# Gathering the last two channel blocks of expert 0's tokens between the two halves of its gate products

## The reference

```python
hdn = (silu(einsum('nd,edf->nef', xt, w_gate[gi])) * einsum('nd,edf->nef', xt, w_up[gi]))
hdn = hdn * comb[:, gi, :, None]          # weight of each token for each expert, mostly zero
y = y + einsum('nef,efd->nd', hdn, w_down[gi])
```

## Time and profile before

| | before |
|---|---|
| median of 3 runs | 772.37 us (772.29 to 773.62) |
| the profiled execution, its own time | 772.13 us |
| its span in the profile | 770.4 us |
| TensorE busy | 750.6 us, 97% of the span |
| weights read | 240.56 MB in all, mean 312 GB/s |
| granted TensorE clock | 0.998 |

### The profile page before, as it was taken

The page is one execution under the profiler, slowest core; times in us unless marked ns, Lnnn a source line. Parts: engine busy times, 40 slices in busy tenths (PEclk is TensorE's granted clock), DMA queues, the critical chain, the costliest instruction groups (busy, mean ns, idle before and its releaser), DMA issues.

```text
span 770.4 us, 16167 instructions
## 1 busy us (share of the span) xinstructions
PE 750.6 (97%) x6544; PEld 538.9 (70%) x6544; DVE 323.0 (42%) x795; ACT 311.6 (40%) x632; POOL 124.9 (16%) x209
## 2 busy tenths in 40 slices
PE   8999999999999999999999999999999999998995
PEld 8989989998999988755555555565555555455552
DVE  4895787678675855712211311221222113012112
ACT  6976678576684744712112121222112121111123
POOL 7473242225423640000000000000000000000000
PEclk9999999999999999999999999999999999999999
DMA  8537554554754479999999999999999999999993
GB/s 206 148 86 194 149 145 131 138 151 111 191 140 125 153 241 327 374 407 421 427 424 430 426 428 427 429 424 428 425 428 427 427 429 424 430 426 428 422 415 127
DMA packets 83265, 240.56 MB, mean 312 GB/s; under 512 B 7281, under 2 KB 65762, under 8 KB 69746
## 3 DMA queue, kind: packets, MB, share of 16 engines
q1 hardware_dynamic: 82882, 238.67, 81.4%
q10 hardware_dynamic: 304, 0.79, 0.4%
HBM read 238.40 MB, written 1.05 MB: 311 GB/s over the span
## 4 chain that ended last, share of the span: by engine, by line
PE 83%; DMA 11%; DVE 3%; issue 2%; ACT 1%; SPq 0%; DVEq 0%
PE banks L2218 24%; PE banks L1863 22%; PE banks L2276 12%; DMA ring<-in_expert_w_up_dram 10%; PE banks L2142 3%; PE banks L2231 3%; PE banks L2060 3%; PE banks L1983 1%; PE banks L1996 1%; PE banks L2252 1%; PE banks L2044 1%; PE banks L2000 1%; PE banks L1987 1%; DMA room<-in_w_in_dram 1%; PE banks L2021 1%
## 5 line engine op out<-in xcount | busy, mean ns | idle before, releaser
L2218 PE MATMUL banks<-ring,bench 128*64 128x256 f32 x2016 | 235.6, 388 | 5.1 <-DMA ring<-in_expert_w_up_dram 3.6
L2218 PEld LDWEIGHTS banks<-ring,bench 128*64 128x64 f32 x2016 | 144.5, 134 | 102.6 <-issue 19.5
L1863 PE MATMUL banks<-rounded 128*128 128x256 f32 (+2 forms) x1320 | 193.5, 293 | 0.4 <-DVE room L1481 0.4
L1863 PEld LDWEIGHTS banks<-rounded 128*128 128x128 f32 x1320 | 168.0, 188 | 3.7 <-issue 0.6
L1762 DVE TENSOR_TENSOR bench<-banks,bench 128x256 f32<-128x256 f32 x32 | 13.6, 424 | 254.3 <-PE banks L2218 182.7
L2276 PE MATMUL banks<-ring,bench 128*64 128x512 f32 x512 | 116.9, 598 | 0.3 <-ACT bench L1144 0.3
L1155 ACT ACTIVATE ysb<-banks 64x512 f32<-64x512 f32 x63 | 37.3, 592 | 150.3 <-PE banks L2276 149.5
L2276 PEld LDWEIGHTS banks<-ring,bench 128*64 128x64 f32 x512 | 33.9, 136 | 62.8 <-issue 60.2
L923 ACT ACTIVATE rounded<-room 128x1024 fp32r<-128x1024 f32 x64 | 67.4, 1054 | 22.1 <-PE banks L1863 15.0
L1144 ACT ACTIVATE bench<-banks 128x256 f32<-128x256 f32 x32 | 12.3, 385 | 142.8 <-PE banks L2252 142.8
L1381 DVE TENSOR_TENSOR rounded<-room,rounded 128x1024 fp32r<-128x1024 f32 x49 | 62.4, 1273 | 15.2 <-ACT rounded L923 14.2
(11 more groups left out here) (317 smaller groups left out, 876.4 us busy)
## 6 DMA issues: line engine op xcount, KB each, us to landing
ring<-in_expert_w_down_dram SPq DMA_DIRECT2D x27, 2048.0 KB, 24.8
ring<-in_expert_w_up_dram SPq DMA_DIRECT2D x25, 2048.0 KB, 26.9
ring<-in_expert_w_gate_dram SPq DMA_DIRECT2D x24, 2048.0 KB, 25.9
room<-in_w_in_dram SPq DMA_DIRECT2D x56, 512.0 KB, 4.0
ring<-in_expert_w_gate_dram SPq DMA_DIRECT2D x10, 1024.0 KB, 9.8
ring<-in_expert_w_up_dram SPq DMA_DIRECT2D x8, 1024.0 KB, 10.4
ring<-in_expert_w_up_dram SPq DMA_DIRECT2D x12, 512.0 KB, 6.5
ring<-in_expert_w_down_dram SPq DMA_DIRECT2D x6, 1024.0 KB, 8.7
```

The lines of the kernel that those rows point to most:

```text
L1863: ins = T.matmul(o, a, b[:, k, lo_at:L], start=(k == 0 and n == 0), stop=(k == KT - 1 and n == 2))
L2218: ins = T.matmul(pb[5 + c][half * 64:half * 64 + SLOTS, 0:256], xgT[:, q % ROOMS, kt, j * SLOTS:(j + 1) * SLOTS], ws[kt // 4][:, kt % 4, h ...
```

## The change

TensorE now runs parts 0 to 2 of the first gather, starts gate 0's products with channel blocks 0 to 3, then gathers part 3, and then runs gate 0's blocks 4 to 7. On VectorE `weigh` goes ahead of `bring(0, 3)`. The number of instructions stays the same, and no semaphore is added or taken away.

```diff
                     bring(0, 1)
+                    weigh()
                     bring(0, 3)
-                    weigh()
                     weighed()
                     settle()
...
                 def gather_first():
...
                             ins = products(xlo, part, t)
                             if t == TT - 1:
                                 ins.then_inc(S("gathered"), 1)
+                def gather_last_part():
+
                     for t in range(TT):
                         products(xhi, PARTS - 1, t)
                     for t in range(TT):
...
                     for kt in range(KT):
+                        if first and c == 0 and kt == KT // 2:
+                            gather_last_part()
                         if first and c == 0 and kt % 4 == 0:
                             pe.wait_ge(S("xgT_side"), kt // 4 * 2 + 2)
```

More of the change, by code:

```diff
@@ L2153, in spread_gain, with products @@
                     ins.then_inc(S("gathered"), 1)
-                def gather_first():
[L2157 to L2165, removed]
+                per = KT // PARTS
+                def products(x, part, t):
+                    for k in range(per):
+                        ch = (part * per + k) * P
+                        ins = T.matmul(pb[FIRST_BANK[part]][:, k * WIDE:(k + 1) * WIDE], x[:, t, ch:ch + P], hot[:, t, :],
+                                       start=(k == 0 and t == 0 and x is xhi), stop=(t == TT - 1 and x is xlo), skip_group_check=True)
+                    return ins
+                def gather_first():
                     for t in range(TT):
```

## The result

The changed kernel takes 773.93 us (median of 22 runs, 772.14 to 774.86), the kernel before 772.47 us (22 runs, 771.99 to 774.21). The ratio is 1.0016, 95% interval 1.0010 to 1.0021: slower by 1.46 us at the medians, which is clear of zero. It is 0.19%, just inside the 0.2% (1.5 us) that the prediction took for the least that can be told from no change, and the interval reaches 0.21%. The forecast was 772.0 us, with a range up to 773.6.

A forecast was written before the change was run, and what follows sets the result against it. The weight stream was taken to bound the end. Profiled 772.13 us less 0.36 for the earlier first release gave 771.8; the runs' median lying 0.24 above the profiled execution made it 772.0 us, range 771.3 to 773.6.

The forecast's parts named there:

- What bounds the kernel: From 340 us on the weight stream sets the end; TensorE delays before 612 us are made up if no hole opens.
- its three cases: Whole-kernel time against 772.37 us: same 0.88 (within 1.5 us), faster 0.05, slower 0.07.
- Gate 0's start and the first release: TensorE starts gate 0 at 322.40 after idling about 0.68 us; half 1 of chunk 9 is issued 0.36 us earlier.
- Gate 0's end: Gate 0 on TensorE ends at 327.22 instead of 326.54, 0.68 us later.
- The wait at kt = 6: Blocks 6 and 7 wait for VectorE's part 3, ready 0.09 us before wanted: cost nothing, 0.85 us if not hidden.
- VectorE: Moved weigh costs nothing; the chain behind bring(0, 3) ends at about 329.4, hidden with 2 us left.
- the clock: Rival at gate 0: idle TensorE drops from 2.4 to 1.2 GHz, giving about 776.3 us; chance 0.04.
- The SP queue: Half 1 of chunk 9 issues 0.36 us earlier, everything behind 0.68 later; the stream still passes 0.36 us to the end.
- the 4.8 us of the first load: Landing time of half 1 of chunk 9, taken as alone in an empty queue; later loads took 6.4 and 6.7.
- My second reading: At half 0 of chunk 10, 2.2 us from issue to full rate leaves a 0.2 us hole, over half the gain.
- My sign of being wrong: Landings of 4.8 us for the halves of chunk 10 would mean that their issue sets the stream.
- the second half's issue sets the stream: Rival at the 329 us hand-over: up to 0.68 us slower, 0.2 more with a VectorE wait, 772.5 to 773.3; chance 0.21.

The follow-up runs named there:

- the long delay: Kernel before with 24 idle gather matmuls put between gate 0's halves: 776.28 us, ratio 1.0048 (1.0032 to 1.0064).

## Why the prediction was wrong

What bounds the kernel was right: the end follows the weight stream, TensorE's own delay before 612 us costs nothing by itself, and the loss of the first 340 us is still there at the end. By the prediction's own bound of 0.2% the result is "same", the likeliest of its three cases, but barely, and not for the reason given; the sign and the time were wrong, and the median lies 0.3 us above the range.

*Gate 0's start and the first release.* Right in kind: 322.44 against 322.40 forecast, the idle 0.62 us against 0.68, the release 0.28 earlier against 0.36.

*Gate 0's end.* Mis-sized: 1.00 us late against 0.68. Gate 0 began 0.78 us after the place where part 3 had begun (322.44 less 321.72 - 0.06, the shift of the traces) where I had 0.68; part 3 took 1.12 us between the halves against 1.04, and each half 1.96 against 1.89. The last two I take for the price of changing once more between gathers and products, which the working left out; no run tests that.

*The wait at kt = 6, VectorE, the clock.* Right: no idle there, `weigh` is free, and PEclk stayed at 1.00 through the 0.62 us. The Trainium skill, "TensorE: Matmul & The Clock Gate" (Part 1), says that the throttled clock is the default and activity releases it; at this pause no fall shows.

*The SP queue.* This is the step that failed: "by its own issue it could land at 327.33 + 4.8", so that the stream would stay the later of the two and "the 0.36 us pass through it to the end". I took the 4.8 us of the first load as the floor for one that follows another, and all above it as waiting that a later issue would use up. I worked that out for three loads, up to half 1 of chunk 10, and went from there to the end. For half 0 of chunk 10, the hand-over that I looked at, the bytes show no loss. By the same rule half 1 of chunk 11, which landed after 6.4 us before, would have had 1.6 us to spare. In its place the runs showed that it had none: with its issue 0.54, 1.00, 1.28 or 3.21 us later, the stream was 0.66, 1.41, 1.67 or 3.17 us later from there on, while releases ahead of it gained nothing by coming earlier. The 4.8 us were not those of a load in an empty queue either: half 0 of chunk 9, issued at 315.37, was still landing until 326.87, two microseconds after half 1 was issued:

```profile
spare<-in_expert_w_gate_dram SPq DMA_DIRECT2D x1, 1024.0 KB, 11.5
```

My second reading, a hole of 0.2 us, looked at the same hand-over. My sign of being wrong, landings of 4.8 us for the halves of chunk 10, did not show in the trace of the change, and the loss came all the same.

*The rivals.* The nearest was "the second half's issue sets the stream", with a chance of 0.21 and a price of up to 0.68 us, 0.9 with the wait. It was right in that late releases behind the first half set the stream. But it looked for that at 329 us, where the trace of the change shows no loss, and its price was bounded by the wrong delay; by the median it is 1.46 us. The rule of the Trainium skill ("DMA: Bandwidth & Descriptors", Specifications: 0.6 us to the first byte) would have kept the hole shut. In the trace of the long delay, where the stream stood still, the first packet begins at 330.46, 0.95 us after the start of the issue's record (329.51, lasting 0.33) and 0.62 after its end, so the rule agrees if it counts from the end. What it does not cover is that the first fifteen packets then take up to 1.23 us each.

Open: why half 1 of chunk 11 takes 5.6 to 6.2 us from its issue to arrive where a load issued into a still stream takes 4.5 (half 0 of chunk 10 with the delay of 24, counted the same way), why the first packets after a pause are slow, and why hand-overs with a lead of 2.4 us (half 0 of chunk 11, issued at 331.69, slow packets from 334.08 on) have slow packets when others with less do not. Loads larger than 1 MB or from another queue were not tried.

## What to carry to other kernels

Where a stream of loads is released by the work that uses them, look for the stretch in which the queue holds little besides the load under way, and in it for the longest pause between two releases. Here a later release there counted in full, while earlier ones gained nothing against the kernel before. Work moved behind a first release to get it out sooner delays all the others, so cost the last release of the stretch, not the first, and follow the sum through every load until the queue has filled up. And the landing time of a load that follows another did not tell its reserve; a delay put in by hand did, at the price of one run, and showed where there is a reserve (here by one expert later).

## What the runs showed of the hardware

A packet of 8 KB took 0.309 us in a full stream and 0.36 to 1.23 us among the first fifteen after the stream had stood still, the first of which began 0.95 us after the start of its issue's record and 0.62 after the end. In the change single packets took up to 2.2 us, while the DMA share of the stretches from 328 to 340 us stayed at 0.95 to 0.97; only GB/s showed it (336 to 358, against 424 before in the last of them). Packets of 4, 8 and 16 KB took 159, 309 and 614 ns at the median. The landing time of the same 1 MB load at the same place differed between traces of the same code by up to 2.5 us (4.8 and 7.3), by its last engine. Part 3 and the two halves of gate 0 each took 0.07 to 0.08 us more once they alternated, without a gap that the page would list.
